# An encoder kernel with earlier row loads, routing on raw rows, a re-paced attention core and a re-ordered recurrence unit

## The chip, the cores and the metric

One Trainium2 chip; the kernel runs on one of its cores. The metric is device time in microseconds of one execution, the median of several runs. PE is TensorE, PEld its weight loads, DVE VectorE, ACT ScalarE, POOL GpSimd, SP the engine that issues most DMAs. The granted clock is the share of TensorE's full 2.4 GHz that the throttle allowed; 0.5 is 1.2 GHz.

## What is computed

Two layers over 512 tokens (two sequences of 256), width 1024, all in fp32. Each layer is a mixer and a mixture of experts, both behind a row normalisation and with a residual.

```python
for i in range(2):
    h = rms_norm(x, norm_mix[i])
    x = x + (recurrent_mixer(h, ...) if i % 2 == 0 else window_attention(h, ...))
    h = rms_norm(x, norm_ffn[i])
    x = x + hier_moe(h, ...)

# recurrent_mixer: one projection, then a gated linear scan (RG-LRU) and a delta-rule scan, each in both directions
state = state * w_t + (state @ -kk_t) (kk_t * a_t) + v_t k_t ;  y_t = state @ r_t     # per head, 64 x 64
# window_attention: 16 query heads on 4 key heads, blocks of 128 queries against 384 keys, a sink logit in the softmax
s = q k * scale + alibi ;  p = softmax([s, sink])[..., :384] ;  o = p v
# hier_moe: 4 groups of 8 experts, top 2 in the best group
group = argmax(x wg1 + bg1) ; top_p, top_e = top_k(softmax((x wg2 + bg2)[group]), 2)
y[token] += weight * (silu(xb w_gate[e]) * (xb w_up[e])) w_down[e]      # 32 experts
```

## The kernel before

All of it is one program with an order written out by hand for every engine; engines meet at semaphores. Tokens stand as four tiles of 128 rows (TT = 4) by 1024 columns in X, which is the residual. Weights stream through a ring of 2 MB slots, issued on SP.

The start. SP issues the four tiles of X (L1187), the first 0.5 MB of the first weight slot (L1199), then under `n == 1` sixteen small vectors (L1193, L1196; the last is mu_r) and a wait until all vectors have landed. PE transposes the vectors (L1933, L1934), then the normalised tiles (L273, `pe_turn_norm`), waits for POOL's masks (`consts_ready`, set at L1277, waited for at L1961), and begins the projection (L1969).

The norms. `pe_turn_norm(pe, j, t)` turns tile t for the j-th norm of the kernel; j = 1 and 3 are the norms ahead of the two expert layers. ACT sums squares (L255) and takes the root (L257), DVE the reciprocal (L261) and the product with the row (L266), PE turns eight 128x128 pieces, ACT (L311) and DVE (L319) copy them out into hT with the weight of the norm. The router multiplies hT by its weights (L656) into 36 logits a token; `fill(4)` (L663) are four matmuls into an unused bank. `dve_moe` picks group and experts (L491 to L519); the rank of each token within its expert is made by 14 matmuls (L672 to L676) from Eany; L546 and L548 turn it into keys, L534 into one-hot matrices, with which `gather` (L687) picks the rows of an expert.

The recurrence. Eight units (4 blocks of heads by 2 directions) follow each other. Each inverts a triangular matrix by blocks: 8x8 blocks first (first_products on PE, L2069; first_masks L1798 to L1800 on DVE; spread_rows L2076 on PE; block_inverse L1810 to L1821 on DVE), then levels 3, 4 and 5, each of which is a product z (L2105), its mask (L1836), a product t (L2114) and a sum (L1844), with transposes between (L2122, L2084, L2129). The unit before is finished in between (turn, rhs, solve, outputs), and rest_products (L2096, masked at L1830) makes the other products. A unit's PE order ends so:

```python
                t(u, 5)
                if u < UNITS - 1:
                    spin(3, 0)
                    turn_blocks(u + 1)
                turn_last(u)
```

`spin` (L2173) multiplies into a bank that nobody reads. turn_blocks(u + 1) needs the last result of block_inverse(u + 1); DVE makes this between level_masks(u, 5) and level_sums(u, 5).

The attention core. Sixteen steps (4 query tiles by 4 key heads, NU = 16). For a step PE makes scores (L963), DVE adds the bias (L1098), takes the maximum (L1102) and three small steps (L1104 to L1106), ACT takes the exponential with its sum (L1045), PE turns the probabilities (L989) into two banks, which ACT (L1053) and DVE (L1112) copy out, one each; PE multiplies them by the values (L1001), DVE divides (L1124). After each fourth step PE turns the output tile (L977) and ACT copies it (L1059). PE's order runs scores one step ahead and the values one step behind, and DVE divides two steps behind. The projection after it is L1015.

The experts: L687, L695, L713, L739, with the weights streaming.

Of the kernel before, what the change touches and what calls it, by code (L numbers as in the profile page):

```python
# [20 lines left out]
P = 128  # L21
# [36 lines left out]
def trunk(nc, a, y_prompt, y_sample):  # L58
    ctx = ExitStack()
    with ctx:  # L60
# [120 lines left out]
        def row(name):  # L181
# [40 lines left out]
        rhs_done, rhs_out, u_done, u_out, ys_done, ys_out, loop_step = (  # L222
            sem(n) for n in ("rhs_done", "rhs_out", "u_done", "u_out", "ys_done", "ys_out", "loop_step"))
# [44 lines left out]
        def pe_turn_norm(pe, j, t):  # L268
            pe.wait_ge(xn_ready, TT * j + t + 1)
            if t >= 2 - j % 2:  # L270
                wait_hT(pe, j, t - 1 + j % 2)
            for c in range(KC):
                mm = nc.tensor.transpose(turn_bank(j, t, c // 4)[:, (c % 4) * P:(c % 4 + 1) * P], XN[j][:, t, c * P:(c + 1) * P], ident[:, :])  # L273
                if c % 4 == 3:
                    mm.then_inc(hT_raw, 1)
# [8 lines left out]
        def dve_out_norm(dve, step, j, done):  # L284
            for t in range(TT):
# [7 lines left out]
                dve_norm(dve, step, j, t)  # L293
            dve_hT(dve, j, TT - 1)

        def act_out_norm(act, j):
            for t in range(TT):
                if t and j % 2:
                    act_hT(act, j, t - 1)
                act.wait_ge(x_updated, 8 * (j - 1) + 2 * t + 2)  # L300
                act_norm_tile(act, j, t)
                if t and not j % 2:
                    act_hT(act, j, t - 1)
            act_hT(act, j, TT - 1)
# [42 lines left out]
        RATE_BANK = (0, 7, 0, 1, 2, 3, 7, 0)  # L347

# [21 lines left out]
        Eany, at = carve(AR, at, [TT, EXPERTS])  # L370
# [126 lines left out]
        def dve_moe(dve, step, l):  # L497
            m = moe[l]
            dve.wait_ge(lg_done, l + 1)
# [166 lines left out]
        def pe_moe(pe, l):  # L666
            m = moe[l]
            fill(4)
            pe.wait_ge(choice_ready, l + 1)
            for t in range(TT):  # L670
                o = bank[3][:, t * EXPERTS:(t + 1) * EXPERTS]
                mm = nc.tensor.matmul(o, chunkmask[:, 0, 0, :], Eany[:, t, :], start=True, stop=(t == 0))  # L672
                for b in range(t):
                    mm = nc.tensor.matmul(o, ones[:, :], Eany[:, b, :], start=False, stop=(b == t - 1))
            for t in range(TT):
                mm = nc.tensor.matmul(bank[3][:, TT * EXPERTS:(TT + 1) * EXPERTS], ones[:, :], Eany[:, t, :],  # L676
                                      start=(t == 0), stop=(t == TT - 1))
            mm.then_inc(rank_done, 1)

# [149 lines left out]
        def pe_over(pe, l):  # L829
# [66 lines left out]
        s_done, s_ready, m_ready, p_ready, p_turned, pT_a, pT_d, o_done, o_ready, o_turned, oT_out = (  # L896
            sem(n) for n in ("s_done", "s_ready", "m_ready", "p_ready", "p_turned", "pT_a", "pT_d", "o_done",
# [20 lines left out]
        def pe_att(pe):  # L918
# [49 lines left out]
            for w in range(NU + 2):  # L968
                if w + 1 < NU:
                    scores(w + 1)  # L970
                if w >= 2 and (w - 2) % KVH == KVH - 1:
                    pe.wait_ge(pT_a, min(w, NU))
                    pe.wait_ge(pT_d, min(w, NU))
                    pe.wait_ge(o_ready, w - 1)
                    t = (w - 2) // KVH
# [4 lines left out]
                if w < NU:  # L980
                    pe.wait_ge(p_ready, w + 1)
                    if w:
                        pe.wait_ge(pT_a, w)
                        pe.wait_ge(pT_d, w)
                    if w >= 2 and (w - 2) % KVH == KVH - 1:
                        pe.wait_ge(oT_out, 2 * ((w - 2) // KVH + 1))
# [5 lines left out]
                if 1 <= w <= NU:  # L992
# [3 lines left out]
                    pe.wait_ge(pT_d, v + 1)  # L996
# [26 lines left out]
        def act_att(act):  # L1023
# [17 lines left out]
            for w in range(NU + 2):  # L1041
# [13 lines left out]
                if w >= 2 and (w - 2) % KVH == KVH - 1:  # L1055
                    t = (w - 2) // KVH
# [12 lines left out]
        def dve_att(dve, step):  # L1069
# [19 lines left out]
            for w in range(NU + 2):  # L1089
                if w < NU:  # L1090
# [12 lines left out]
                    sink = bb[:, 4 * j:4 * j + 4]  # L1103
                    step(nc.vector.scalar_tensor_tensor(s_[:, 0, :], s_[:, 0, :], SCALE, sink, ALU.mult, ALU.max))  # L1104
                    step(nc.vector.tensor_scalar(s_[:, 1, :], s_[:, 0, :], -1.0, None, ALU.mult))
                    nc.vector.tensor_tensor(s_[:, 4, :], sink, s_[:, 1, :], ALU.add).then_inc(m_ready, 1)  # L1106
                if 1 <= w <= NU:
                    v = w - 1
                    par = v % 2
                    s_ = st[:, par, :, :]  # L1110
                    dve.wait_ge(p_turned, v + 1)
                    nc.vector.tensor_copy(pT[:, par, 4:8, :].rearrange("p a b -> p (a b)"), bank[5][:, :]).then_inc(pT_d, 1)  # L1112
                    if v >= 2:
                        dve.wait_ge(o_ready, v - 1)
                    step(nc.vector.tensor_tensor(s_[:, 5, :], s_[:, 2, :], s_[:, 3, :], ALU.add))
                    step(nc.vector.reciprocal(s_[:, 5, :], s_[:, 5, :]))
                if w >= 2:
                    v = w - 2
# [1191 lines left out]
```

## Time and profile before

| | us |
|---|---|
| median of 3 runs | 1934.21 (1932.78 to 1935.5) |
| the profiled execution | 1931.3 |
| its span, first to last instruction | 1929.5 |
| start, until the first projection matmul | 24.95 |
| recurrence units, 228.22 to 499.67 | 271.45 |
| expert layer of layer 0, after its routing | 458.09 |
| attention core, first score matmul to output projection | 109.70 |

The profile is of one execution. Times in it count from the first instruction. An idle time stands before the instruction that ended it, with the one that released it.

### The profile page before, as it was taken

To read this page: it belongs to the slowest core of one execution; us is meant where nothing else is said; L and a number is where in the kernel's file an instruction comes from. 1 tells how busy PE (TensorE), PEld (TensorE's weight loads), DVE (VectorE), ACT (ScalarE), POOL (GpSimd) and SP (SyncE) were. 2 spreads that over 40 slices of the span, in tenths; PEclk is the share of its full clock that TensorE was granted. 3 is DMA by queue.
4 is the path that set the end of the run, shared out by engine and by line. 5 is a ranking of instruction groups with operands and counts; after the bars stand their busy time and mean duration, and the time that the engine had idled before them with its cause. 6 is when DMAs were issued, how large, how long until landed. Compare 5 with 4: busy or idle time off the path is not lost.

```text
span 1929.5 us, 22747 instructions
## 1 busy us (share of the span) xinstructions
PE 1812.6 (94%) x9052; PEld 880.3 (46%) x9052; DVE 676.8 (35%) x1285; ACT 446.8 (23%) x924; POOL 71.6 (4%) x110
## 2 busy tenths in 40 slices
PE   6999999999898999999999989778989999999998
PEld 3434478878554333333333344676543333333333
DVE  3159687776324111111111245673241111111114
ACT  3284323223421111111111132452111111111111
POOL 4130000000000000000000200000000000000001
PEclk9999899999998999999999999887989999999999
DMA  8000000001242999999999872100049999999997
GB/s 294 6 0 1 1 1 2 2 1 45 88 174 88 376 427 430 428 428 429 429 428 429 352 270 87 44 1 1 0 174 396 429 428 429 429 429 429 427 429 295
DMA packets 68230, 460.95 MB, mean 239 GB/s; under 512 B 18700, under 2 KB 19846, under 8 KB 43590
## 3 DMA queue, kind: packets, MB, share of 16 engines
q1 hardware_dynamic: 56118, 435.90, 54.4%
q10 hardware_dynamic: 9744, 15.77, 2.2%
q0 software_dynamic: 2304, 8.39, 1.3%
q8 instruction: 44, 0.72, 0.2%
q14 instruction: 20, 0.16, 0.0%
HBM read 442.21 MB, written 17.83 MB: 238 GB/s over the span
## 4 chain that ended last, share of the span: by engine, by line
PE 80%; DVE 10%; ACT 5%; issue 2%; DMA 2%; SPq 0%; POOL 0%; DVEq 0%; ACTq 0%; POOLq 0%
PE bank L713 21%; PE bank L739 12%; PE bank L687 11%; PE bank L1969 5%; PE bank L936 4%; PE bank L1015 3%; PE bank L2260 3%; PE bank L695 2%; ACT hT L459 2%; PE bank L2105 2%; PE bank L2114 1%; PE bank L2096 1%; PE bank L1001 1%; PE bank L273 1%; PE bank L1952 1%
## 5 line engine op out<-in xcount | busy, mean ns | idle before, releaser
L713 PE MATMUL bank<-ring,arena 128*64 128x512 f32 x2048 | 450.4, 592 | 1.6 <-DVE arena L539 1.6
L606 DVE TENSOR_TENSOR arena<-arena,bank 64x512 f32<-64x512 f32 x64 | 68.3, 1067 | 626.0 <-ACT arena L467 625.9
L713 PEld LDWEIGHTS bank<-ring,arena 128*64 128x64 f32 x2048 | 146.8, 137 | 293.4 <-issue 291.3
L687 PE MATMUL bank<-arena 128*64 128x512 f32 x1024 | 234.1, 599 | 7.3 <-DVE arena L606 4.9
L739 PE MATMUL bank<-ring,arena 128*64 128x512 f32 x1024 | 239.4, 610 | 0.9 <-ACT arena L471 0.9
L1969 PE MATMUL bank<-hT,ring 128*128 128x512 f32 x336 | 147.8, 600 | 5.7 <-ACT arena L1425 4.0
L687 PEld LDWEIGHTS bank<-arena 128*64 128x64 f32 x1024 | 73.8, 138 | 155.2 <-issue 128.8
L467 ACT ACTIVATE arena<-bank 64x512 f32<-64x512 f32 x64 | 37.9, 592 | 401.1 <-PE bank L713 401.1
L739 PEld LDWEIGHTS bank<-ring,arena 128*64 128x64 f32 x1024 | 69.2, 139 | 125.7 <-issue 124.5
L539 DVE TENSOR_TENSOR arena<-bank,gffn 128x512 f32<-128x512 f32 x64 | 44.3, 692 | 187.1 <-PE bank L695 187.1
L1969 PEld LDWEIGHTS bank<-hT,ring 128*128 128x128 f32 x336 | 64.3, 192 | 87.9 <-issue 87.9
L479 ACT ACTIVATE arena<-bank 128x512 f32<-128x512 f32 x64 | 38.2, 597 | 264.8 <-PE bank L739 264.8
L459 ACT ACTIVATE hT<-bank 128x512 f32<-128x512 f32 x64 | 38.2, 597 | 202.5 <-PE bank L687 202.5
L936 PE MATMUL bank<-hT,ring 128*128 128x512 f32 x160 | 72.2, 606 | 1.3 <-issue 1.3
L647 POOL DMA_INDIRECT xn<-expert_rows,dest x16 | 18.6, 1163 | 1372.3 <-DMA expert_rows<-arena 1364.2
L695 PE MATMUL bank<-ident,hT 128*128 128x128 f32 x256 | 42.6, 289 | 20.4 <-ACT hT L459 19.6
L1015 PE MATMUL bank<-ring,hT 128*128 128x512 f32 x128 | 57.6, 606 | 1.2 <-ACT hT L1059 1.2
L2260 PE MATMUL bank<-ring,xn 128*128 128x512 f32 x128 | 57.8, 605 | 0.0
L936 PEld LDWEIGHTS bank<-hT,ring 128*128 128x128 f32 x160 | 31.1, 195 | 40.6 <-issue 40.6
L2105 PE MATMUL bank<-ring 128*128 128x128 f32 x384 | 48.9, 280 | 0.5 <-ACT ring L1499 0.5
L1080 DVE RECIPROCAL arena<-arena 128x512 f32<-128x512 f32 x10 | 33.5, 3353 | 43.4 <-ACT arena L1066 43.3
L2114 PEld LDWEIGHTS bank<-ring,Zb 128*128 128x128 f32 x384 | 45.4, 192 | 6.8 <-issue 5.9
(368 smaller groups left out, 1977.4 us busy)
## 6 DMA issues: line engine op xcount, KB each, us to landing
ring<-in_moe_w_gate_dram SPq DMA_DIRECT2D x64, 2048.0 KB, 10.3
ring<-in_moe_w_up_dram SPq DMA_DIRECT2D x64, 2048.0 KB, 15.0
ring<-in_moe_w_down_dram SPq DMA_DIRECT2D x64, 2048.0 KB, 12.5
expert_rows<-arena ACTq DMA_DIRECT2D x120, 128.0 KB, 8.2
ring<-in_rec_w_in_dram SPq DMA_DIRECT2D x5, 2048.0 KB, 12.8
ring<-in_att_w_in_dram SPq DMA_DIRECT2D x3, 2048.0 KB, 8.6
ring<-in_rec_w_out_dram SPq DMA_DIRECT2D x2, 2048.0 KB, 8.4
ring<-in_att_w_out_dram SPq DMA_DIRECT2D x2, 2048.0 KB, 19.2
```

Source lines behind the costliest of these rows:

```text
L459: nc.scalar.activation(xt, bank[2][:, :], ACT.Copy).then_inc(m["xt_ready"], 1)
L606: nc.vector.tensor_tensor(hb[0:CAP, par, :].rearrange("s (f p) -> s p f", f=4), sg[0:CAP, par, :].rearrange("s (p f) -> s p f", f=4), bank ...
L687: mm = nc.tensor.matmul(bank[2][h * CAP:(h + 1) * CAP, :], onehot[:, par, t, :], xm[:, t, h * 512:(h + 1) * 512], start=(t == 0), stop=(t ...
L695: mm = nc.tensor.transpose(bank[3][:, k * P:(k + 1) * P], xt[:, k * P:(k + 1) * P], ident[:, :])
L713: mm = nc.tensor.matmul(bank[par][k * CAP:(k + 1) * CAP, :], xg[:, par, c, :], W[k][:, c * FF:(c + 1) * FF], start=(c == 0), stop=(c == KC ...
L739: mm = nc.tensor.matmul(bank[6 + par][h * CAP:(h + 1) * CAP, :], hT2[:, par, f, :], W[2][:, f * D + h * 512:f * D + (h + 1) * 512], start= ...
L936: mm = nc.tensor.matmul(bank[2 + i % 4][:, :], W[:, c, (i % 4) * P:(i % 4 + 1) * P], hT[:, c, :], start=(c == 0), stop=(c == KC - 1))
L1015: mm = nc.tensor.matmul(bank[4 + i % 4][:, :], hT[:, c, t * P:(t + 1) * P], W[:, c, :], start=(c == 0), stop=(c == KC - 1))
L1969: mm = nc.tensor.matmul(o, W[:, c, (f % 4) * P:(f % 4 + 1) * P], hT[:, c, :], start=(c == 0), stop=(c == KC - 1))
L2105: mm = nc.tensor.matmul(bank[q][:, i * P:(i + 1) * P], Mb[u % 2][:, p, 0, :], Tb[u % 2][:, p, 0, :], start=True, stop=True)
L2114: mm = nc.tensor.matmul(bank[2 + q][:, i * P:(i + 1) * P], Zb[:, p, :], Tb[u % 2][:, p, 1, :], start=True, stop=True)
L2260: mm = nc.tensor.matmul(bank[4 + i % 4][:, :], mixT[:, c, (i // 2) * P:(i // 2 + 1) * P], W[i % 2][:, c, :], start=(c == 0), stop=(c == KC ...
```

## The change

Four parts in one kernel.

Rows: the small vectors are issued before the first weight slot, not behind it. SP's wait for them stays where it was.

Routing: for j = 1 and 3 PE turns the raw rows of X, not the normalised ones, reading every eighth column of a row as one piece; the factor of the norm (rstd) is multiplied into the logits. ACT and DVE copy the last turned tile out before they normalise it. The normalised rows are needed by `gather` alone, which gets a wait for them. The ranks are made by 5 wider matmuls instead of 14; Eany gets a zero block behind it.

Attention core: scores run two steps ahead, the division runs three steps behind, ACT copies both banks of turned probabilities, and the three small steps on DVE become two (the sink is negated once ahead of the loop).

Recurrence unit: the spins go. first_products of the next unit moves from behind t(u, 4) to behind t(u, 3); its masks and rows follow on DVE before level 4, the substitution after the sums of level 4, its blocks after the masks of level 5; the spread rows are copied out of their bank by ACT (`rows_copy`). rest_products 1 to 3 move back by one place each. exp_factors moves from the head of ACT's unit to its end, a unit earlier. Unit 7 keeps its old order.

```diff
             for n in range(6):
-                if n == 1:
+                if n == 0:
                     for name, r in ROWS[7:]:
...
+                if n == 1:
                     sp.wait_ge(vec_loaded, 16 * 19)
...
         def pe_turn_norm(pe, j, t):
-            pe.wait_ge(xn_ready, TT * j + t + 1)
+            if j % 2:
+                pe.wait_ge(x_updated, 8 * (j - 1) + 2 * t + 2)
+            else:
+                pe.wait_ge(xn_ready, TT * j + t + 1)
...
+                src = X[:, t, :].rearrange("p (q c) -> p c q", c=KC)[:, c, :] if j % 2 else XN[j][:, t, c * P:(c + 1) * P]
...
             dve_hT(dve, j, TT - 1)
+            dve_norm(dve, step, j, TT - 1)
...
             step(nc.vector.tensor_tensor(lg, bank[2][:, 0:144].rearrange("p (t e) -> p t e", t=TT),
-                                         bb[:, b:b + 36].unsqueeze(1).to_broadcast([P, TT, 36]), ALU.add))
+                                         rstd[:, 0:TT].unsqueeze(2).to_broadcast([P, TT, 36]), ALU.mult))
+            step(nc.vector.tensor_tensor(lg, lg, bb[:, b:b + 36].unsqueeze(1).to_broadcast([P, TT, 36]), ALU.add))
...
+            nc.tensor.matmul(bank[3][:, 0:(TT + 1) * EXPERTS], chunkmask[:, 0, 0, :], Eany0.rearrange("p t e -> p (t e)"),
+                             start=True, stop=False)
             for t in range(TT):
...
+                mm = nc.tensor.matmul(bank[3][:, (t + 1) * EXPERTS:(TT + 1) * EXPERTS], ones[:, :],
+                                      Eany[:, t, :].unsqueeze(1).to_broadcast([P, TT - t, EXPERTS]),
+                                      start=False, stop=(t == TT - 1))
             mm.then_inc(rank_done, 1)
+
+            pe.wait_ge(xn_ready, TT * (2 * l + 2))
...
             scores(0)
-            for w in range(NU + 2):
-                if w + 1 < NU:
-                    scores(w + 1)
+            scores(1)
+            for w in range(NU + 3):
+                if w + 2 < NU:
+                    scores(w + 2)
...
-                    nc.scalar.activation(pT[:, v % 2, 0:4, :].rearrange("p a b -> p (a b)"), bank[4][:, :],
-                                         ACT.Copy).then_inc(pT_a, 1)
+                    for c in range(2):
+                        ins = nc.scalar.activation(pT[:, v % 2, 4 * c:4 * c + 4, :].rearrange("p a b -> p (a b)"),
+                                                   bank[4 + c][:, :], ACT.Copy)
+                    ins.then_inc(pT_a, 1)
...
-                    nc.vector.tensor_copy(pT[:, par, 4:8, :].rearrange("p a b -> p (a b)"), bank[5][:, :]).then_inc(pT_d, 1)
...
+            def rows_copy(u):
+                act.wait_ge(f_done, 3 * u + 3)
+                nc.scalar.activation(R8.rearrange("p k a j -> p (k a j)"), bank[6][:, :], ACT.Copy).then_inc(b6_out, 1)
...
                 if nxt is not None:
+                    ready(0, 1, 2)
+                    level_masks(u, 3)
+                    ready(3, 4, 5)
+                    rest_masks(u, 0)
+                    level_sums(u, 3)
                     first_masks(nxt)
+                    first_products_out(nxt)
+                    first_rows(nxt)
+                    level_masks(u, 4)
+                    rest_masks(u, 1)
+                    level_sums(u, 4)
+                    substitute(nxt)
+                    rest_masks(u, 2)
+                    level_masks(u, 5)
+                    blocks_out(nxt)
+                    rest_masks(u, 3)
+                    level_sums(u, 5)
...
                 t(u, 3)
-                rest_products(u, 1)
+                if u < UNITS - 1:
+                    first_products(u + 1)
+                else:
+                    rest_products(u, 1)
                 turn_level(u, 3)
...
                 z(u, 4)
+                if u < UNITS - 1:
+                    rest_products(u, 1)
                 if u:
                     outputs(*prev, 0)
-                rest_products(u, 3)
+                if u < UNITS - 1:
+                    spread_rows(u + 1)
+                else:
+                    rest_products(u, 3)
                 t(u, 4)
                 if u:
                     rhs(*prev, 1)
                 if u < UNITS - 1:
-                    first_products(u + 1)
+                    rest_products(u, 2)
...
                 t(u, 5)
                 if u < UNITS - 1:
-                    spin(3, 0)
                     turn_blocks(u + 1)
                 turn_last(u)
```

## Rows read from the trace of the kernel before

**Rows 1.** The page: the span; busy us, share of it and instructions of each engine.

```profile
span 1929.5 us, 22747 instructions
...
PE 1812.6 (94%) x9052; PEld 880.3 (46%) x9052; DVE 676.8 (35%) x1285; ACT 446.8 (23%) x924; POOL 71.6 (4%) x110
```

**Rows 2.** Stretches: length, busy of each engine (instructions), granted clock, DMA share, GB/s.

```profile
0.00:24.95 24.95, 6.69 (x35) 6.16 (x35) 8.21 (x19) 12.58 (x31) 21.05 (x58) 1.00 0.82 298
...
228.22:255.42 27.20, 23.64 (x177) 18.16 (x177) 25.00 (x53) 6.21 (x10) 0.00 (x0) 1.00 0.00 1
255.42:463.76 208.34, 204.69 (x1908) 171.64 (x1908) 159.75 (x321) 63.66 (x136) 6.22 (x9) 1.00 0.03 11
...
1227.23:1240.62 13.39, 9.29 (x41) 7.05 (x41) 8.67 (x24) 6.07 (x20) 0.00 (x0) 0.63 0.27 115
...
1227.23:1336.93 109.70, 87.07 (x545) 75.87 (x545) 70.72 (x192) 48.01 (x169) 0.00 (x0) 0.78 0.04 15
```

**Rows 3.** Chain of waits, first 30 us: start, length, what.

```profile
6.89 8.27 DMA arena<-in_rw_mu_r_dram
...
24.95 5.39 PE bank L1969 x12
```

**Rows 4.** Timeline, first 32 us: start, length, instruction.

```profile
13.14 0.30 ACT L257 ACTIVATE rstd<-ssq,small 128x1 f32<-128x1 f32 x1
...
20.71 0.10 POOL L1277 MEMSET small<- 128x1 f32 x1
```

**Rows 5.** DMA issues, first 40 us: count, size, issue to landing.

```profile
X<-in_x_sample_dram SPq DMA_DIRECT2D x2, 512.0 KB, 6.0
```

**Rows 6.** PE timeline, the projection before and after an idle time.

```profile
125.55 9.61 PE L1969 MATMUL bank<-hT,ring 128*128 128x512 f32 x22
...
141.11 9.10 PE L1969 MATMUL bank<-hT,ring 128*128 128x512 f32 x16 [4.05 <-ACT arena L1425]
```

**Rows 7.** One unit as a stretch (columns as in rows 2).

```profile
290.17:324.87 34.70, 34.02 (x317) 28.39 (x317) 27.19 (x55) 10.39 (x23) 1.46 (x2) 1.00 0.00 1
```

**Rows 8.** Timeline of all engines, end of that unit.

```profile
320.38 2.74 PE L2173 MATMUL bank<-chunkmask,ident 128*128 128x512 f32 x6
...
323.53 1.28 DVE L1844 TENSOR_TENSOR ring<-bank,ring 128x512 f32<-128x512 f32 x2
...
324.87 1.14 PE L2129 MATMUL bank<-ident,ring 64*64 64x64 f32 x16 [0.54 <-DVE ring L1844]
```

**Rows 9.** PE timeline, routing of layer 0.

```profile
593.83 1.09 PE L273 MATMUL bank<-ident,arena 128*128 128x128 f32 x8 [1.96 <-DVE arena L266]
596.31 3.60 PE L656 MATMUL bank<-wr,hT 128*128 128x36 f32 x16 [1.39 <-ACT hT L311]
...
607.94 1.06 PE L676 MATMUL bank<-arena,ones 128*128 128x32 f32 x8
610.22 6.59 PE L687 MATMUL bank<-arena 128*64 128x512 f32 x16 [1.22 <-DVE arena L534]
```

**Rows 10.** PE timeline, routing of layer 1.

```profile
1419.98 3.65 PE L687 MATMUL bank<-arena 128*64 128x512 f32 x16 [1.22 <-DVE arena L534]
```

**Rows 11.** PE timeline, attention core.

```profile
1272.02 1.94 PE L989 MATMUL bank<-ident,xn 128*128 128x128 f32 x8 [2.28 <-ACT arena L1053]
...
1291.48 1.09 PE L989 MATMUL bank<-ident,xn 128*128 128x128 f32 x8
1292.41 1.90 PE L1001 MATMUL bank<-arena 128*128 128x64 f32 x16
1294.24 1.13 PE L963 MATMUL bank<-arena 64*128 64x256 f32 x8
```

**Rows 12.** Groups of the core by line: count, busy, mean ns, idle before.

```profile
L1112 DVE COPY arena<-bank 128x512 f32<-128x512 f32 x16 | 11.0, 687 | 7.6 <-PE bank L989 7.6
L1053 ACT ACTIVATE arena<-bank 128x512 f32<-128x512 f32 x16 | 9.2, 577 | 1.3 <-PE bank L989 1.3
```

**Rows 13.** One line's durations over its twelve instructions, ns (min/median/max).

```profile
L266 DVE TENSOR_SCALAR arena<-X,rstd x12: 753/1146/1156, 546.5 to 1402.2; 128x1024 f32<-128x1024 f32 x12
```

More of the change, by code:

```diff
@@ L299, in act_out_norm @@
                     act_hT(act, j, t - 1)
+                if t == TT - 1 and j % 2:
+                    act_hT(act, j, t)
                 act.wait_ge(x_updated, 8 * (j - 1) + 2 * t + 2)
@@ L303, in act_out_norm @@
                     act_hT(act, j, t - 1)
-            act_hT(act, j, TT - 1)
+            if not j % 2:
+                act_hT(act, j, TT - 1)
         def act_hT(act, j, t):
@@ L498, in dve_moe @@
             m = moe[l]
+            step(nc.vector.memset(Eany0[:, TT, :], 0.0))
             dve.wait_ge(lg_done, l + 1)
@@ L1040, in act_att @@
                 nc.scalar.activation(KD[0:HD, j, :], kraw[lo:lo + HD, j // 2, :], ACT.Copy).then_inc(att_kd, 1)
-            for w in range(NU + 2):
+            for w in range(NU + 3):
                 if w < NU:
@@ L1088, in dve_att @@
             dve.wait_ge(att_kd, 8)
-            for w in range(NU + 2):
+            step(nc.vector.tensor_scalar(bb[:, 0:HEADS], bb[:, 0:HEADS], -1.0, None, ALU.mult))
+            for w in range(NU + 3):
                 if w < NU:
@@ L1102, in dve_att @@
                     step(nc.vector.tensor_reduce(s_[:, 0, :], S_, AX.X, ALU.max))
[L1103 to L1111, printed above, removed]
-                    nc.vector.tensor_copy(pT[:, par, 4:8, :].rearrange("p a b -> p (a b)"), bank[5][:, :]).then_inc(pT_d, 1)
[L1113 to L1118, printed above, removed]
+                    nsink = bb[:, 4 * j:4 * j + 4]
+                    step(nc.vector.scalar_tensor_tensor(s_[:, 1, :], s_[:, 0, :], -SCALE, nsink, ALU.mult, ALU.min))
+                    nc.vector.tensor_tensor(s_[:, 4, :], s_[:, 1, :], nsink, ALU.subtract).then_inc(m_ready, 1)
+                if w >= 3:
+                    v = w - 3
                     t, j, par = v // KVH, v % KVH, v % 2
@@ L1126, in dve_att @@
                                             s_[:, 5, :].unsqueeze(2).to_broadcast([P, 4, HD]), ALU.mult).then_inc(o_ready, 1)
+                if 1 <= w <= NU:
+                    v = w - 1
+                    par = v % 2
+                    s_ = st[:, par, :, :]
+                    dve.wait_ge(p_ready, v + 1)
+                    if v >= 2:
+                        dve.wait_ge(o_ready, v - 1)
+                    step(nc.vector.tensor_tensor(s_[:, 5, :], s_[:, 2, :], s_[:, 3, :], ALU.add))
+                    step(nc.vector.reciprocal(s_[:, 5, :], s_[:, 5, :]))
             dve_out_norm(dve, step, 3, att_out_done)
@@ L1545, in unit_copies @@
                     output_copies(*prev, 0)
+                if u < UNITS - 1:
+                    rows_copy(u + 1)
+                if u:
                     rhs_copy(*prev, 1)
@@ L1552, in unit_copies @@
                     output_copies(*prev, 1)
+                if u < UNITS - 2:
+                    exp_factors((u + 2) // 2, (u + 2) % 2)
                 if u < UNITS - 1:
@@ L1559, in _ @@
                 rate_sigmoid(v)
+            exp_factors(0, 1)
             block_turned(0)
@@ L2091, in rest_products @@
                     pe.wait_ge(m_out, 8 * u + 2 * c)
+                if c == 1 and u < UNITS - 1:
+                    pe.wait_ge(f_out, 3 * u + 5)
                 for k in range(2):
@@ L2200, in unit @@
                 if u < UNITS - 1:
-                    first_products(u + 1)
+                    rest_products(u, 2)
                 else:
@@ L2209, in unit @@
                 z(u, 5)
+                if u < UNITS - 1:
+                    rest_products(u, 3)
                 if u:
                     outputs(*prev, 1)
-                if u < UNITS - 1:
-                    spread_rows(u + 1)
-                else:
+                if u == UNITS - 1:
                     gn_gate(0)
```

114 lines of the change are left out of this document (56 added, 58 removed).

## The prediction

> **What bounds the kernel now.** The page first: PE is busy for 1812.6 of 1929.5 us [rows 1], so time is to be had where PE idles, where it runs at half clock, or where its work goes away. Next the table of stretches with the granted clock [rows 2]: in the attention core PE is busy for 87.07 of 109.70 us at a mean clock of 0.78; the start has 6.69 us of PE work in 24.95; the recurrence units are full (204.69 of 208.34, clock 1.00), so there only work can go. Then the PE timeline of each place, to see what ended its idle times. The expert layers are left alone by the change, and I count nothing for them. The sums go against the profiled execution (1931.3, span 1929.5); the median of the runs is 2.9 above it, which I add at the end.
>
> **Start.** The chain waits for mu_r, issued at 6.89 behind a 0.5 MB piece of weights and landed 8.27 later, and PE's first projection matmul comes at 24.95 [rows 3], 9.8 after it landed. Issued ahead of the weights, these rows stand behind the tiles of X only, whose last half lands 6.0 after its issue [rows 5]; I put their landing at 8.5 to 9, an estimate. SP's wait for them stays behind the first slot piece, which lands some 2 to 3 us later (13.5 to 14) and is not late for anything. Next is ACT's fourth root, over at 13.44 [rows 4], which puts the last transposes at 16 to 18.4. But PE also waits for POOL's masks, whose mark is set at 20.81 [rows 4] and doesn't move. So the projection starts at 20.9, 4.05 earlier. PE then idles for 3 to 5 us ahead of it. After an idle time of 4.05 sixteen such matmuls took 9.10, where 22 in a row took 9.61, or 6.99 for sixteen [rows 6]: 2.1 us lost to half clock. Net **-2.0**, between 0 and -4.1.
>
> **Recurrence.** A unit is 34.70 us with 34.02 of PE [rows 7]. What goes: the three spins, 2.74 from 320.38, and the 0.54 of idle in front of turn_last, where PE waits for L1844 [rows 8]. Both exist because DVE makes the substitution of the next unit between the masks and the sums of level 5. In the new order that chain starts some 9 us sooner, behind t(u, 3), and turn_blocks finds it done. 34.70 less 3.28 is 31.42 of PE; DVE is busy for 27.19 in a unit [rows 7], loses nothing but a few reads of a bank, and gets 4 us of room. ACT is busy for 10.39 and takes on the copy of the rows (0.6, like L1053 [rows 12]). I laid the new order out by hand with these durations: PE stays full, but with little to spare. The second rhs waits for rows_copy (0.4 to 0.5 us of slack), rest_products 3 for the masks of rest 2 (0.5), spread_rows for first_rows (0.6), t(u, 4) for its masks (0.2 to 0.8), turn_last for the sums (0.35), turn_blocks for blocks_out (1.4). Each of these is a new wait with all of PE's queue behind it. Six units (1 to 6) gain 3.1 to 3.3 (the spins are 2.6 to 2.8 by unit), 18.7 to 19.9. Unit 0 has no older unit to weave in: it is bound by DVE (25.00 of 27.20 [rows 2]) and its chain is as long as before; I count +0.5 for a longer idle time in it. Moving exp_factors(0, 1) ahead of block_turned(0) costs ACT some 2.5 us in a stretch where it works for 6.21 of 27.20 [rows 2]: nothing; without that cover it would be 2.5 once. Unit 7 keeps its order. Net **-18.0**; -13 if every unit misses by another us, -19.5 at best.
>
> **Routing.** Layer 0: PE waits 1.96 for the normalised tile, 1.39 for the copies, then runs the router at half clock (3.60 for 16 [rows 9], so 1.8 at full clock). Raw rows can be turned as soon as the residual is added, 1.96 sooner, the second wait stays, and the router comes to full clock; the logits are ready about 2.2 sooner, after one more DVE step of 0.3. The ranks: 28 instructions (fourteen fp32 matmuls, two each) at 0.13 (1.06 for 8 [rows 9]) are 3.3 us; ten wider ones are 1.2 to 1.8: another 1.5 to 2. The extra wait before gather is for DVE's last norm, which I have at 597.5 against a gather at 606: nothing. Together -3.9. Layer 1 gains as much up to its ranks, but there the first gather ran at full clock, 3.65 [rows 10], against 6.59 in layer 0 [rows 9], and PE will now stand idle for 3.6 before the ranks, so I charge 3: -1.1. If it stays at full clock, -4.3.
> Against this stand the strided loads: the 64 transposes of the two norms read every eighth column. No PE row shows that; on DVE one line takes 0.753 where its source is contiguous and 1.146 where it is strided by eight [rows 13], a factor of 1.52. Eight transposes take 1.04 (8.3 for 64). At +52% that is +4.3; the loads may hide beside the matmuls, or double the time: 0 to +8. I take **+3.2**, nearer the DVE row. The Trainium skill (Advanced Engine Details and Errata, SBUF Cachelines) speaks against this edit: it says that accesses which each touch another 16-byte line pay a penalty, and it gives no size; the stride here is 32 bytes. Rows 13 agree for DVE, and no row here shows it for PE.
> Net of routing **-1.8** (-8 to +4).
>
> **Attention core.** With PE dense, a step is transposes 0.93, values 1.83, scores 1.13 [rows 11], 3.9 us. DVE is busy 70.72 / 16 = 4.4 a step [rows 2]; it loses the copy (0.687 [rows 12]) and one step of 0.17, which leaves 3.6, or 3.95 with the gaps between dependent steps. ACT is busy 3.0 and gets one copy of 0.58: 3.6. So all three engines need 3.85 to 3.95, and the second step of lead on the scores and the later division take the waits off PE's path (2.28 at 1272.02, after which PE ran at half clock [rows 11]: 1.94 for 8 transposes, against 1.09). ACT's second copy is new on PE's path: values(v) waits for 1.16 of copies instead of 0.6, with scores between to cover it. Each fourth step adds the output transposes and the wait for ACT's copies, about 2.05. First transposes at 1234.8 as before; fifteen steps of 3.85, 1.6 to fill the pipe, three times 2.05: the last begins at 1300.3; 7.4 more for values, division, transposes and copies: output projection at 1307.7 instead of 1336.93, -29.2. It starts at full clock, another -1.7 (as in the 2.1 of rows 6). Against this, the idle time of 4 us ahead of the first transposes stays, and the clock is at 0.63 there now [rows 2]; 5.6 us at half clock cost 2.9. Net **-28**; the best is -31, and -18 if DVE's step stays at 4.5.
>
> **Sum**: -2.0 - 18.0 - 1.8 - 28.0 = -49.8, so 1881.5 for a profiled execution and **1884** for the median.
>
> **Rivals.**
> (a) The clock still falls in the core. Its 87.07 us of PE are 65 at full clock, so half clock costs 22 us there now; three new idle times of 1.3 stand behind the output transposes, and one of 2.28 was enough once [rows 11]. If 18 of the 22 remain, 1902. For it: the core has only short bursts. Against: the dense step from 1291.48 to 1294.24 stayed at full clock [rows 11]. The Trainium skill (TensorE: Matmul & The Clock Gate, Part 4: PE-mode transpose) bears on this: it says transposes do not count as activity for the clock as matmuls do, and a quarter of the new step is transposes. Rows 11 show transposes at full clock, between matmuls.
> (b) The new order of the unit leaves PE waiting for DVE: the slacks of 0.2 to 0.6 are gone and half the gain with them, 1884 + 9 = 1893. For it: six tight waits; against: DVE has 4 us of room in a unit.
> (c) The strided loads cost twice or more: 5 to 8 us above the sum, 1889 to 1892.
> (d) All goes as at best, no clock loss at the start and in layer 1: 1872 to 1876.
> (e) Slower than before: without spins the clock falls in the units and stays low. 31.4 us of PE at full clock are 62.8 at half, so a unit costs 31.4 more, and 50 / 31.4 = 1.6 units at half clock eat all that the change gains; from two on the kernel is slower: two give 1884 + 63 = 1947, six 2072. Place: unit 0, with 2.35 us of idle in a row by my layout. Against: units now run at 1.00 [rows 2] and 34.02 of 34.70 busy, and without spins 31.3 of 31.4.
>
> **How the numbers follow.** The forecast (1876 to 1892): 0.60. (a) 0.15. (b) 0.10. (c) 0.06. (d) 0.05. (e) 0.04, of which 0.01 near no change. The range from 1872 to 1904 covers the first five and the bounds of the unknown terms. A measurement of this kernel can tell about 0.2% (3.9 us) from no change. Faster by more than that 0.95, within it 0.01, slower 0.04.
>
> **What would show it.** First projection matmul at 20.9, PE idle before it for 3 to 5 us. Periods of turn_last at 31.4 for units 1 to 6, no DVE releaser in front of it above 0.2. Router of both layers at 1.9, not 3.60; eight transposes of the raw rows at 1.04 or, if strides count, up to 2. Core of 80 us with a mean clock above 0.95 behind its first 6 us and steps of 3.9. I am wrong if the clock in the core stays near 0.8, if a unit takes 33 us or more, or if the expert layers move.

## The result and the profile after

The changed kernel takes 1864.57 us (median of 4 executions, 1863.17 to 1875.53), the kernel before beside it 1934.54: a ratio of 0.9655, interval 0.9619 to 0.9690, faster by 70 us. On a second chip it was 1865.32 against 1931.19 (0.9666, 0.9632 to 0.9699), faster by 66. The forecast was 50 faster, 1884, with a range from 1872: the direction was right, every part of the change gains, and the size lies outside the range.

The profiled execution of the changed kernel happens to be its slowest, 1875.5. I therefore profiled it once more (e1 below, 1864.2) and read both. The parts, each from one mark of PE's timeline to the next, in us (z is the first product of a unit, turn_last its last transpose; the token transposes follow the first gather):

| part, from mark to mark | forecast | before | after | after, e1 |
|---|---|---|---|---|
| start: until z of unit 0 | -2.0 | 228.22 | 226.64 | 227.92 |
| units 0 to 6: z of unit 0 to turn_last of unit 6 | -18.0 | 235.54 | 214.50 | 214.48 |
| routing, layer 0: third router tile to the first token transposes | -3.9 + 1.6 | 27.61 | 20.21 | 20.07 |
| core: first scores to the projection behind it | -28 with the next row | 109.70 | 86.96 | 80.01 |
| that projection, to the third router tile of layer 1 | | 62.64 | 64.21 | 61.28 |
| routing, layer 1 | -1.1 + 1.6 | 24.80 | 19.91 | 21.61 |
| span | | 1929.5 | 1873.7 | 1862.5 |

(The 1.6 are the halves of the 3.2 charged for strided loads.) What remains of the span's difference lies behind unit 7 and in the first two and the last expert of each layer: nothing in the first profile, 3.9 us less in e1. An expert in the middle of a layer takes 15.24 in both kernels.

Stretches of the profile after, first the start, unit 0, units 1 to 6 and one unit, then the core: length, busy us of PE, PEld, DVE, ACT and POOL (instructions), granted clock, DMA share, GB/s.

```profile
0.00:21.58 21.58, 6.89 (x35) 6.41 (x35) 8.24 (x19) 13.80 (x32) 18.66 (x53) 0.99 0.93 336
226.64:252.99 26.35, 20.80 (x171) 17.21 (x171) 24.22 (x52) 4.74 (x9) 0.00 (x0) 1.00 0.00 1
252.99:441.14 188.15, 187.87 (x1872) 165.66 (x1872) 159.84 (x321) 65.07 (x140) 7.83 (x9) 1.00 0.04 13
284.48:315.70 31.22, 31.13 (x311) 27.40 (x310) 26.86 (x55) 10.82 (x24) 1.45 (x2) 1.00 0.01 2
1194.73:1207.30 12.57, 9.68 (x49) 7.02 (x50) 9.45 (x26) 7.83 (x26) 0.00 (x0) 0.67 0.29 124
1194.73:1281.69 86.96, 77.30 (x544) 67.85 (x545) 58.34 (x161) 55.59 (x185) 0.00 (x0) 0.84 0.05 19
1264.30:1281.69 17.39, 15.61 (x72) 15.05 (x73) 1.62 (x5) 5.16 (x15) 0.00 (x0) 0.50 0.00 1
```

Against [rows 2, 7]: units 1 to 6 are 188.15 instead of 208.34, PE idle in them for 0.3 us in all, at full clock. DVE works as long as before in a unit (26.86, 27.19 before), only no longer in PE's way. The core's last 17 us ran at half clock in this execution.

The start, on PE's timeline: mu_r lands at 10.58 instead of 15.16 [rows 3], the projection begins at 21.58 instead of 24.95, and what it waits for now is POOL's mark, as forecast, followed by half clock (8.67 for 16, 6.99 at full [rows 6]).

```profile
10.58 0.39 PE L1973 MATMUL bank<-ident,arena 96*128 96x96 f32 x1 [10.58 <-DMA arena<-in_rw_mu_r_dram]
...
21.58 8.67 PE L2009 MATMUL bank<-hT,ring 128*128 128x512 f32 x16 [2.68 <-POOL small L1291]
```

The end of a unit, to be held against [rows 8]: t(u, 5), turn_blocks, turn_last without a gap between them.

```profile
281.63 2.05 PE L2161 MATMUL bank<-ring,Zb 128*128 128x128 f32 x16
283.51 1.04 PE L2129 MATMUL bank<-ident,ring 128*128 128x128 f32 x8
284.48 1.14 PE L2176 MATMUL bank<-ident,ring 64*64 64x64 f32 x16
```

The routing of layer 0, against [rows 9]: router (L670), transposes of the raw rows (L277), fills (L677), ranks (L684, L687), gather (L701).

```profile
565.68 1.87 PE L670 MATMUL bank<-wr,hT 128*128 128x36 f32 x16
567.38 1.12 PE L277 MATMUL bank<-ident,X 128*128 128x128 f32 x8
569.89 2.71 PE L670 MATMUL bank<-wr,hT 128*128 128x36 f32 x16 [1.39 <-ACT hT L320]
572.40 6.30 PE L677 MATMUL bank<-ones,ident 128*128 128x512 f32 x8
578.79 0.54 PE L684 MATMUL bank<-arena,chunkmask 128*128 128x160 f32 x2
579.17 0.97 PE L687 MATMUL bank<-arena,ones 128*128 128x128 f32 x8
581.45 3.65 PE L701 MATMUL bank<-arena 128*64 128x512 f32 x16 [1.31 <-DVE arena L548]
```

The 1.96 of idle ahead of the transposes is gone, the ranks take 1.4 and not 3.3, and the gather runs at full clock, 3.65 and not 6.59. Note the fills: 6.30, mostly at half clock (3.68 at full, in e12), so that they last until the ranks. In layer 1 of this profile the router ran at full clock (1.95), and of the fills a part still did not:

```profile
1351.83 5.38 PE L677 MATMUL bank<-ones,ident 128*128 128x512 f32 x8
1358.81 0.54 PE L684 MATMUL bank<-arena,chunkmask 128*128 128x160 f32 x2 [1.60 <-DVE arena L533]
```

### The profile page after: what moved, and what is told of

The parts are those of the page before. It is cut to its first block, busy times and chain, and to the rows that moved or that the text cites. A ratio compares the mean times of both kernels' runs of the same rounds, so it can differ in the third digit from the quotient of the medians.

```text
span 1873.7 us, 22602 instructions
## 1 busy us (share of the span) xinstructions
PE 1776.7 (95%) x8974; PEld 860.5 (46%) x8974; DVE 665.1 (35%) x1258; ACT 457.4 (24%) x947; POOL 74.4 (4%) x110
## 4 chain that ended last, share of the span: by engine, by line
PE 85%; DVE 6%; ACT 5%; issue 2%; POOL 1%; DMA 1%; DVEq 0%; ACTq 0%; POOLq 0%
PE bank L727 22%; PE bank L753 12%; PE bank L701 11%; PE bank L2009 6%; PE bank L950 4%; PE bank L1027 3%; PE bank L2315 3%; PE bank L709 2%; PE bank L2152 2%; PE bank L2161 2%; ACT hT L471 2%; PE bank L2143 1%; PE bank L1013 1%; PE bank L1992 1%; PE bank L2062 1%
## 5 line engine op out<-in xcount | busy, mean ns | idle before, releaser
L701 PE MATMUL bank<-arena 128*64 128x512 f32 x1024 | 231.6, 593 | 7.4 <-DVE arena L620 4.9
L701 PEld LDWEIGHTS bank<-arena 128*64 128x64 f32 x1024 | 73.5, 137 | 153.0 <-issue 129.2
L709 PE MATMUL bank<-ident,hT 128*128 128x128 f32 x256 | 42.5, 289 | 20.4 <-ACT hT L471 19.5
L2161 PE MATMUL bank<-ring,Zb 128*128 128x128 f32 x384 | 48.1, 278 | 0.0
## 6 DMA issues: line engine op xcount, KB each, us to landing
ring<-in_moe_w_down_dram SPq DMA_DIRECT2D x64, 2048.0 KB, 12.2
ring<-in_att_w_out_dram SPq DMA_DIRECT2D x2, 2048.0 KB, 20.1
```

The costliest lines, as they stand in the source:

```text
L701: mm = nc.tensor.matmul(bank[2][h * CAP:(h + 1) * CAP, :], onehot[:, par, t, :], xm[:, t, h * 512:(h + 1) * 512], start=(t == 0), stop=(t ...
L709: mm = nc.tensor.transpose(bank[3][:, k * P:(k + 1) * P], xt[:, k * P:(k + 1) * P], ident[:, :])
L2161: mm = nc.tensor.matmul(bank[2 + q][:, i * P:(i + 1) * P], Zb[:, p, :], Tb[u % 2][:, p, 1, :], start=True, stop=True)
```

## The experiments

All edits are against the changed kernel unless said. Medians are held against 1865.3 of e1 (the kernel before: 1931.2, 1931.6 and 1933.1 in the three groups of runs).

**e1, the changed kernel again.** No edit.

> The changed kernel once more, for a second profile. Theory A (the clock in the last steps of the attention core differs between executions): the profiled execution of the changed kernel took 1875.5, the others 1863 to 1866, and in its trace the core runs at a granted clock of 0.50 from 1264 to 1282 and at 0.83 until 1300, which costs 8.7 + 3 = 11.7 us. Then a profile of an execution near 1864 shows this stretch at 0.95 or more, and all else alike within 1 us. Theory B (the difference lies in the experts or in DMA): the stretch is at half clock again also in an execution near 1864.

Profiled 1864.2; all executions 1860.14 to 1871.78. The core took 80.01, and its last steps, in the trace of e1 first and of the first profile second:

```profile
1260.72 1.09 PE L991 MATMUL bank<-ident,xn 128*128 128x128 f32 x8 [1.02 <-ACT arena L1066]
1263.08 1.06 PE L1002 MATMUL bank<-ident,xn 128*128 128x128 f32 x8 [1.27 <-ACT hT L1073]
```

```profile
1261.94 1.09 PE L991 MATMUL bank<-ident,xn 128*128 128x128 f32 x8 [1.02 <-ACT arena L1066]
1264.30 1.94 PE L1002 MATMUL bank<-ident,xn 128*128 128x128 f32 x8 [1.27 <-ACT hT L1073]
1266.03 3.52 PE L1013 MATMUL bank<-arena 128*128 128x64 f32 x16
```

The same two waits (1.02 and 1.27, the first in which no scores are left to cover them), and the clock falls behind them in one execution and not in the other. That is 6.95 us in the core and 2.93 in the projection. Theory A holds for this stretch; "all else within 1 us" does not: the start differs by 1.3 and the gather of layer 1 by 1.7 in the other direction, and the experts of the two layers by 2.4 and 1.8 in the same.

**e2, the old attention core.** The hunks of the core undone: scores one step ahead, division two behind, DVE copying one bank.

> The changed kernel with the attention core of the kernel before, all else as changed. Theory A (core worth what the trace shows with its clock held, 22.7 + 11.7 = 34, less 1.6 of projection): 1864.6 + 32 = 1897. My recorded term (28): 1892. If the clock of the core isn't what differs between executions: 1864.6 + 21 = 1886.

1894.7: the core is worth 29.4. In this trace it takes 106.26 at a mean clock of 0.82, with PE busy for 82.42; e1's has 80.01 at 0.94:

```profile
1192.25:1298.51 106.26, 82.42 (x545) 71.61 (x545) 70.62 (x192) 48.10 (x169) 0.00 (x0) 0.82 0.04 15
```

```profile
1193.52:1273.53 80.01, 70.25 (x544) 60.88 (x544) 58.27 (x161) 55.47 (x185) 0.00 (x0) 0.94 0.05 20
```

Both the theory's 32 and the recorded 28 are near. PE's idle time went from 23.8 to 9.8 (length less busy), and 12.2 of busy time went with the half clock.

**e3, the old routing.** Its hunks undone: normalised rows turned, 14 rank matmuls.

> The changed kernel with the routing of the kernel before (normalised rows turned, 14 rank matmuls). Theory A (the trace: 7.4 gained in layer 0, of which 2.9 is the first gather at full clock, and 4.9 in layer 1): 1864.6 + 12.3 = 1877. My recorded term (1.8): 1866.5. Transposes of eight pieces take 1.04 with either source if strides cost nothing.

1878.9, 13.6 slower: my recorded term of 1.8 was wrong by far. The marks of layer 0 are 27.5 apart, as in the kernel before. Those of layer 1 are 27.5 apart as well, where the kernel before has 24.80: both first gathers ran at half clock here (6.48 and 6.65), so that some 3 us of what the old routing takes in this trace are a gather that ran at full clock in the trace of before. The transposes: eight of them take 1.09 here from contiguous rows and 1.12 above from the strided ones. The price of the stride is in the weight loads, and it is hidden (durations in ns, min/median/max; the changed kernel's, then those of the kernel before):

```profile
L277 PEld LDWEIGHTS bank<-ident,X x64: 186/189/256, 524.7 to 1348.3; 128*128 128x128 f32 x64
L277 PE MATMUL bank<-ident,X x64: 272/274/338, 525.1 to 1348.5; 128*128 128x128 f32 x64
```

```profile
L273 PEld LDWEIGHTS bank<-ident,arena x96: 137/141/226, 549.0 to 1404.1; 128*128 128x128 f32 x96
L273 PE MATMUL bank<-ident,arena x96: 272/273/418, 549.5 to 1404.2; 128*128 128x128 f32 x96
```

A load of strided rows (L277) takes 189 instead of 141, its matmul 274 as before (273), and the loads run beside the matmuls. The page cited in the prediction (the Trainium skill, Advanced Engine Details and Errata, SBUF Cachelines) is right that the access costs more; on PE it costs nothing on the path here.

**e4, the old order of the unit**, with its spins and all.

> The changed kernel with the recurrence order of the kernel before, spins and all. Theory A (the trace: turn_last of unit 7 lies 22.6 earlier, 1.6 of it from the start; 21 from the units): 1864.6 + 21 = 1885.6, with 1.7 more if the half clock behind unit 7 comes back. My recorded term (18): 1882.6.

1893.9, with executions from 1882.5 to 1900.1. The trace has the period at 34.7 for units 1 to 6 and turn_last of unit 7 20.7 later than the changed kernel, as theory A says; the median is 8 beyond it. In the profiled execution (1898.5) the core took 86.8, so the fall of e1's second trace was in it; how many of the others had it is not known, so what the remaining 8 are is open, and I take the 20.7 of the trace for the worth of the units.

**e5, the kernel before without its spins.**

```diff
                 if u < UNITS - 1:
-                    spin(3, 0)
                     turn_blocks(u + 1)
```

> The kernel before, with the three spins of each unit taken out and nothing else moved. Theory A (the spins only fill the time in which DVE makes the last sums; the gain of the new order is DVE's chain leaving PE's path): the period of turn_last stays at 34.7, with 3.3 us of idle in it, and the kernel stays within 3 us of 1931 as long as the clock holds. Theory B (the spins themselves are the cost): 32.0 a unit, 7 x 2.74 = 19 faster, 1912. Recorded rival (e), the clock: the idle brings half clock in the units; each unit of 31 us that ran at half clock would cost up to 31, the period would be well above 35 and the kernel slower than 1931.

1951.7 against 1931.6: 20 us slower (ratio 1.0101, 1.0072 to 1.0129). A unit, and what stands at its end:

```profile
256.53:294.29 37.76, 34.82 (x314) 30.70 (x315) 26.09 (x54) 10.75 (x24) 0.61 (x1) 0.91 0.00 1
```

```profile
292.58 1.17 PE L2084 MATMUL bank<-ident,ring 128*128 128x128 f32 x8 [2.40 <-DVE ring L1821]
294.29 1.96 PE L2129 MATMUL bank<-ident,ring 64*64 64x64 f32 x16 [0.54 <-DVE ring L1844]
296.18 3.78 PE L2105 MATMUL bank<-ring 128*128 128x128 f32 x16
```

turn_blocks still waits for L1821: theory B is out. But the wait isn't free either: behind 2.40 and 0.54 of idle PE runs at half clock for some 6 us (turn_last 1.96 instead of 1.14, z 3.78 instead of 2.05), in every unit, 37.5 to 37.8 a unit. The spins of the kernel before earned 3 us a unit by holding the clock. This is the recorded rival (e) in part: without the spins the clock does fall, but it comes back within each unit. It stayed away from the changed kernel, whose units have no such wait.

**e6, the changed kernel with the spins put back** (the same line, in its old place).

> The changed kernel with the three spins put back ahead of turn_blocks, nothing else. Theory A (in the new order PE is the bound of units 1 to 6): each of them costs 2.74 in full, period 31.3 + 2.7 = 34.0 for these, 6 x 2.7 = 16 for the kernel plus up to 2.7 in unit 0: 1865 + 17 = 1882. Theory B (DVE's chain still ends the unit and the spins fit in the wait): period 31.3, 1865.

1883.0, 17.7 slower. A unit is 33.80:

```profile
315.66 2.05 PE L2161 MATMUL bank<-ring,Zb 128*128 128x128 f32 x16
317.55 2.74 PE L2220 MATMUL bank<-chunkmask,ident 128*128 128x512 f32 x6
320.13 1.04 PE L2129 MATMUL bank<-ident,ring 128*128 128x128 f32 x8
321.10 1.14 PE L2176 MATMUL bank<-ident,ring 64*64 64x64 f32 x16
```

Theory A: the unit is bound by PE, and a period is 2.6 longer (33.80 against 31.22) for 2.6 of work put into it. With e5: the new order and the removal of the spins gain together; the removal alone loses 20.

**e7, fills in the last waits of the core.**

```diff
+                if w == NU - 2:
+                    pe.wait_ge(s_ready, 4 * (NU - 1))
+                    hold(1)
                 if w >= 3 and (w - 3) % KVH == KVH - 1:
...
                     mm.then_inc(o_turned, 1)
+                    if w >= NU - 2:
+                        hold(1)
```

> The changed kernel with four single matmuls into a score bank that nobody reads any more, in PE's waits of the last steps of the attention core (1.0, 1.3, 0.6 and 1.2 us). Theory A (whether the clock falls in these waits is what spreads the executions from 1860 to 1875): granted clock 0.95 or more from the last output tile to the projection in every execution, core 80 us, times between 1860 and 1867, median 1863. If the spread comes from elsewhere it stays, median 1865.

1864.6, executions 1862.83 to 1868.55: the spread is half of e1's, the median the same. The core took 79.86. Over the profiled executions with the new core and without such fills it took 80.0, 79.8, 79.9, 80.0 (e1, e3, e6, e10), 87.0, 86.8, 87.0 (the first, e4, e9) and 92.5 (e11, below, mostly in its first steps); with them 79.9, 81.3 and 78.7 (e7, e8, e12). The fall in the last steps, four times in eight without fills (the first, e4, e9, e11), did not come in the three traces with them. That is in favour of theory A, but three traces are few, and the spread of the times does not settle it: e8, with the same fills, spreads from 1861.38 to 1875.91. What decides the fall without fills is not known. It goes with how the core begins: in the four traces with it the first eight transposes took 1.09 to 1.41 and the second eight had waited 0.6 to 1.1 us for ACT; in the four without it the first eight took 1.97, at half clock, and the second had not waited.

**e8, fills in three more waits**: ahead of the first projection matmul (3), behind the low-rank products at 133 (4), and at the start of the core (3 and 2).

> As e7, and fills as well in three other waits of PE: 2.7 ahead of the first projection matmul, 4.0 in the projection at 135, 2.9 and 2.7 at the start of the attention core. Theory A (half clock behind these waits costs 1.7, 2.1 and some 3.3): 1863 - 7 = 1856. Theory B (what follows is bound by something else, so that a faster clock there only lengthens the next wait): 1863.

1862.9 (1861.38 to 1875.91): theory B. The projection did start at full clock, but it met the next wait sooner, for ACT, with columns as in the timelines above:

```profile
137.55 7.10 PE L2023 MATMUL bank<-hT,ring 128*128 128x512 f32 x16 [0.40 <-ACT arena L1452]
...
155.35 1.22 PE L2005 MATMUL bank<-arena 32*128 32x512 f32 x2 [0.67 <-ACT X L1403]
157.78 2.90 PE L2023 MATMUL bank<-hT,ring 128*128 128x512 f32 x3 [1.22 <-ACT X L1403]
```

Unit 0 begins at 228.45 there, 1.8 later than in the first profile and 0.5 later than in e1. Neither e7 nor e8 can be told from the changed kernel (ratios to before 0.9663, 0.9660 and 0.9655).

**e9, the 14 rank matmuls** in the new routing.

> The changed kernel with the 14 rank matmuls of the kernel before, all else of the routing as changed. Theory A (the trace: 1.85 from the ranks to the gather in each layer): 1865 + 3.7 = 1868.7, the rest of the routing's 12 is the earlier turn and the clock. Rival: the ranks are nearly all of it, 1865 + 10 = 1875.

1876.8 (1868.04 to 1880.95). In the trace the time from the third router tile to the gather is 17.62 and 17.47 in the two layers, 1.85 and 1.95 above the first profile of the changed kernel: 3.8, theory A. The rest of the 11 is not the ranks: in the profiled execution the core took 87.0 with its projection at 64.2. As a time the run is inconclusive.

**e10, one fill and not four** behind the router.

> The changed kernel with one fill behind the router and not four, so that PE stands idle for 3 to 5 us ahead of the ranks. Theory A (the recorded step was right that such an idle time puts ranks and first gather at half clock, and wrong only in that it doesn't come about, since the fills themselves run at half clock and last until the ranks): gather 6.6 and not 3.65 in both layers, ranks 2.5 and not 1.4, 1865 + 7 = 1872. Theory B (idle ahead of the ranks has no bearing on the gather): 1865.

1872.3 (1867.99 to 1883.05). Layer 0:

```profile
570.88 2.05 PE L677 MATMUL bank<-ones,ident 128*128 128x512 f32 x2
577.59 0.90 PE L684 MATMUL bank<-arena,chunkmask 128*128 128x160 f32 x2 [4.66 <-DVE arena L533]
578.29 1.75 PE L687 MATMUL bank<-arena,ones 128*128 128x128 f32 x8
581.35 6.63 PE L701 MATMUL bank<-arena 128*64 128x512 f32 x16 [1.31 <-DVE arena L548]
```

Layer 1 shows the same (4.45 of idle, gather 6.54). Theory A: behind such an idle time ranks and gather do run at half clock. The recorded step had the mechanism right; the idle time it reckoned with did not come about.

All fourteen traces together, with two layers each, bear it out. Where PE had no idle time ahead of the ranks, the first gather took 3.65 (eleven layers, two of them with the old routing). Behind 0.7 to 1.6 us of idle it took 3.65 three times and 5.0 to 6.65 ten times, behind 3.3 to 4.7 us (e10, e12) 4.4 to 6.6 all four times.

**e11, the old place of the vectors' loads.**

> The changed kernel with the small vectors issued behind the first weight slot as before. Theory A (the trace: first projection matmul 3.3 later, half of it given back by its clock): first matmul at 24.9, 1865 + 1.5 = 1866.5. If the idle time ahead of the projection costs nothing: 1868.

1872.3 (1865.11 to 1882.95); as a time it is inconclusive, since the core of the profiled execution (1882.95) took 92.5. That core is of interest by itself: behind a wait of 1.11 its clock stayed at half for 24 us of steps in which PE had no idle time (7.2 a step, not 3.85).

```profile
1209.46 1.94 PE L1002 MATMUL bank<-ident,xn 128*128 128x128 f32 x8 [1.11 <-ACT arena L1066]
1211.19 3.52 PE L1013 MATMUL bank<-arena 128*128 128x64 f32 x16
...
1231.07 1.97 PE L1002 MATMUL bank<-ident,xn 128*128 128x128 f32 x8
1232.83 2.46 PE L1013 MATMUL bank<-arena 128*128 128x64 f32 x16
```

In the trace the projection begins at 25.33, and unit 0 at 228.68, 2.0 later than in the first profile. Unit 0 begins at 228.2, 229.3 and 228.7 in the three traces with the old place that were marked there, and between 223.9 and 227.9 in the ten with the new one and no fills ahead of it, 226.2 in the mean: 2.5 for the rows, from few traces.

**e12, e7 with fills ahead of the last router tile and of the first gather.**

> As e7, and one fill each in PE's 1.3 us waits ahead of the last router tile and ahead of the first gather. Theory A (these short waits decide the clock of router and gather, 3 to 6 us in an execution where it falls): router 1.87 and gather 3.65 in both layers, median 1861. Theory B: as e7, 1864.6.

1867.7 (1866.40 to 1872.91): neither. In layer 0 of its trace the router runs at full clock, and so do the fills behind it, which are therefore over too soon:

```profile
569.75 1.95 PE L670 MATMUL bank<-wr,hT 128*128 128x36 f32 x16 [0.52 <-ACT hT L320]
571.53 3.68 PE L677 MATMUL bank<-ones,ident 128*128 128x512 f32 x8
578.51 0.90 PE L684 MATMUL bank<-arena,chunkmask 128*128 128x160 f32 x2 [3.30 <-DVE arena L533]
579.20 1.75 PE L687 MATMUL bank<-arena,ones 128*128 128x128 f32 x8
580.77 2.06 PE L677 MATMUL bank<-ones,ident 128*128 128x512 f32 x2
582.75 4.44 PE L702 MATMUL bank<-arena 128*64 128x512 f32 x16
```

The ranks start where they did (12.97 behind the third router tile, 13.11 in the first profile; DVE sets that), after 3.30 of idle and at half clock. In layer 1 the idle time is 3.30 too; the ranks kept full clock there, the fill and the gather (4.50) behind them did not. This is the course that the prediction had in mind, and it shows that DVE, not PE, is the bound between router and ranks.

## Why the prediction was wrong

**Routing** is the step that failed: -1.8 forecast, -12.3 in the first profile, -10.7 in e1, 13.6 by e3. The steady part of it is the time from the third router tile to the first gather: 20.1 to 20.5 us in all traces with the old routing, 15.5 to 15.8 with the new one (16.4 once, in e11; e9, e10 and e12, which change this stretch, left out), 4.5 to 4.9 a layer. The rest is the clock of the gather. Three terms failed.

The strided loads, +3.2: nothing to speak of (eight transposes 1.12 instead of 1.09). I took the ratio of a DVE row for PE and let most of it onto the path; the rows under e3 show 48 ns more a load, all beside a matmul of 274. A load of 189 beside such a matmul was no term of the sum.

The charge of 3 for a first gather at half clock in layer 1: the idle time of 3.6 before the ranks was worked out from a router and fills at full clock. The fills ran at half clock in part or for the most part (6.30 in layer 0 behind a router of 2.71, 5.38 in layer 1 behind one of 1.95), and the idle time was 0.1 and 1.6. That such an idle time takes the gather to half clock holds (e10), and 3.3 of it do come about where the fills are at full clock (e12); what failed is that the sum took the fills to be at full clock. (The -1.1 is also not the sum of its parts: 4.3 less 3 is 1.3, and the 3.9 of layer 0 less 3 is 0.9.)

The gather of layer 0, left at half clock as before: it came back to full in both profiles, another -2.9, with PE's idle time ahead of the ranks, 0.91 before, gone. The trace of the kernel before had shown as much: its layer 1, with no idle time there, has its gather at 3.65. The gain is not a sure one (5.35 in e4, e6, e7 and e11, all behind 1.6 of idle). It was in no bound, and so is part of why even the best case, 4.1 + 19.5 + 8 + 31 = 62.6 or 1872, fell short of the measured 66 to 70. The named terms (logits 2.2 sooner, ranks 1.5 to 2) were right in kind and a little low: the ranks of layer 0 begin 2.6 sooner and take 1.9 less.

**Recurrence**: mechanism right, size a little low. Units 1 to 6 gained 20.2, at 31.36 a unit, where the prediction worked out 31.42, 18.7 to 19.9 in all, and then took 18.0; e6 shows that PE is the bound now; all of the six tight waits together come to 0.3 of idle in the six units of the first profile. Unit 0 was 0.85 shorter and not 0.5 longer. Rival (b) did not come. Rival (e) came in e5, at 3 us a unit, and not in the changed kernel.

**Attention core**: steps of 3.8 to 3.9 and 80.0 from the first scores to the projection were forecast (80.5) and measured in e1 (80.01). The 2.9 charged for half clock in the first steps was wrong. Those steps did run at half clock (0.67 until 1207), but their length was set by DVE and ACT anyway: the first rounds of transposes of e1 start 4.0 and 4.9 apart, against 3.85, so 1.2 is lost, and that is in the 80.01. From the first scores to the last steps the first profile and e1 took the same 69.6 us, although their clocks differ in the first of them. So -31 with the projection, not -28. Rival (a) is true of some executions: the clock falls in the last steps and costs 7 us in the core and 3 behind it (the first profile), and once (e11) it stayed at half through 24 us of dense first steps. The execution of the first profile, with the fall, lies inside the forecast's range (1875.5), and that of e1, without it, below; six of the eight timed ones took 1860 to 1867. That the median came out below the range thus hangs in part on a clock that nothing in the prediction could tell. In most of the core it holds (0.98 from 1207 to 1264 in the first profile, although a quarter of PE's work there is transposes). The page cited for that rival (the Trainium skill, TensorE: Matmul & The Clock Gate, Part 4: PE-mode transpose) says that the full clock does not engage for transposes; it does not speak of a mix like this one. The 24 us of e11 would be in line with it, the same steps of the other traces are not.

**Start**: right in mechanism and size. Vectors landed 10.58 (8.5 to 9 forecast), first matmul 21.58 (20.9), then half clock as forecast; -2.5 in the mean of the traces against -2.0. The half clock is not certain either: in e6, e7 and e10 the projection began at full clock behind the same wait (2.5 to 2.8 us), and unit 0 at 223.9 to 225.3; in the seven others at 226.4 to 227.9.

The sum, mended: start -2.5, units -21.0, routing -11, core and projection -31 (or -21 where the clock falls), is -65.5, and the measured 66 to 70 leave up to 4.5. Some of it may lie behind unit 7: from its turn_last to the third router tile it is 93.2 us in the kernel before and 90.6 to 91.6 in ten of twelve traces of the changed kernel and its variants. But e10 and e11 have 93.2 again, and e5, with the old order, has 91.5, so that the change cannot be said to have earned it. In the experts no steady gain is to be read: from the token transposes of layer 0 to the core it is 609.6 before and 605.9 to 611.2 in the twelve. The rest is open.

## What to carry to other kernels

Follow the clock through filler work as well: fills at half clock last twice as long (2.05 for one in e10, 1.02 in e12) and may close the very gap that you charge for; at full clock (e12), or with fewer of them (e10), it stays open. Fillers in a wait can be worth more than they cost: here 20 us in the old order, and minus 18 in the new one, so take the wait away first and the fillers after it. Before you charge a slower weight load, look whether it runs beside a matmul that is longer. And take more than one profile: two of the same kernel were 11 us apart here.

## What was not expected of the hardware

The granted clock can differ behind the same idle times: 1.02 and 1.27 us ahead of the last output tiles left it at full in four profiled executions of kernels with the new core and took it to half in four others, which makes 9.9 us of difference between the two profiles of the changed kernel. And once at half it can stay there through 24 us without an idle time (e11), where the units of e5 were back at full after some 6. Idle times of 2.40 and 0.54 us in e5 brought 6 us at half clock in each unit, while in the core of the kernel before the same 2.28 us ahead of transposes took the clock to half once (at 1272.02, 1.94 for eight) and left it at full another time (at 1297.65, 1.06).
